# Load gates that register no readers, scratch stores on GpSimd's queue, transposes on SP's queue alone, and scale rows spread from columns

## The reference

```python
h = rmsnorm(x, norm1_g)
z = h @ w_in                       # 1536 columns: a (pool) | u | v
a = z[:, :512]; u = gelu(z[:, 512:1024]); v = gelu(z[:, 1024:])
pool = einsum((trailing_mean(a, windows 2/4/8/16) - a), pool_w) * pool_scale
gate = u * (masked(gmlp_ws) @ v + gmlp_b)      # chunks of 128 positions
x = x + concat(pool, gate) @ w_out
f = rmsnorm(x, norm2_g) @ w_up                 # 4096 columns
x = x + square(relu(f)) @ w_down
y = rmsnorm(x, normf_g)
```

## Time and profile before

| | us |
|---|---|
| median of 3 runs | 1406.8 (1393.67 to 1419.03) |
| the profiled execution | 1400.45 |
| span of its slowest core (core 2) | 1398.9 |
| spans of the 8 cores | 1372.8 to 1398.9 |
| PE busy | 1245.1 (89% of the span) |
| DVE, ACT, POOL busy | 556.3, 377.9, 47.0 |

### The profile page before, as it was taken

One profiled execution on the slowest core, in us unless ns is written; L12 is line 12 of the kernel. 1 busy time (PEld: TensorE's weight loads), 2 busy tenths in 40 slices (PEclk: granted clock), 3 DMA queues, 4 the chain that ended last, 5 costly groups with the idle time before them and its releaser, 6 DMA issues.

```text
span 1398.9 us, 18963 instructions; the slowest of 8 cores (1372.8 to 1398.9 us)
## 1 busy us (share of the span) xinstructions
PE 1245.1 (89%) x6628; PEld 648.8 (46%) x6628; DVE 556.3 (40%) x1165; ACT 377.9 (27%) x735; POOL 47.0 (3%) x91
## 2 busy tenths in 40 slices
PE   1688850499999999999999999999999999999996
PEld 0343420245545545545545545544554554554552
DVE  1764410234445336435435434442542443362312
ACT  0233200112224224223323323322431431421311
POOL 1010000000000000000000000000000000000000
PEclk6698975699999999999999999999999999999998
DMA  7996899847458349469448449549538637747751
GB/s 159 196 244 167 67 116 26 138 113 167 133 153 303 154 139 255 151 190 277 151 145 279 163 145 262 181 144 239 204 143 228 217 137 221 195 152 207 251 211 46
DMA packets 104605, 247.16 MB, mean 177 GB/s; under 512 B 70592, under 2 KB 70784, under 8 KB 81728
## 3 DMA queue, kind: packets, MB, share of 16 engines
q1 hardware_dynamic: 82224, 191.12, 44.4%
q0 software_dynamic: 12784, 52.47, 16.5%
q10 hardware_dynamic: 9504, 2.36, 5.8%
HBM read 218.07 MB, written 34.43 MB: 181 GB/s over the span
## 4 chain that ended last, share of the span: by engine, by line
PE 82%; another core or an unknown queue 4%; DVE 4%; DMA 3%; ACTq 3%; issue 2%; ACT 1%; SPq 1%; DVEq 0%; POOL 0%; POOLq 0%
PE ps L756 26%; PE ps L738 25%; PE ps L447 8%; PE ps L621 7%; PE ps L700 6%; PE ps L720 5%; PE ps L481 4%; ACTq L341 3%; DMA WAU<-w_au 1%; DMA H2T<-HB 1%; DMA RING<-xt 1%; ACT JUNK L306 1%; PE ps L576 1%; DVE X L779 0%
## 5 line engine op out<-in xcount | busy, mean ns | idle before, releaser
L738 PE MATMUL ps<-H2T,RING 128*128 128x384 bf16 x2304 | 387.6, 326 | 1.2 <-ACT ST L742 0.7
L756 PE MATMUL ps<-RING,ST 128*128 128x512 bf16 x1728 | 374.9, 379 | 0.0
L738 PEld LDWEIGHTS ps<-H2T,RING 128*128 128x128 bf16 x2304 | 224.1, 98 | 149.6 <-issue 2.0
L756 PEld LDWEIGHTS ps<-RING,ST 128*128 128x128 bf16 x1728 | 169.0, 98 | 202.5
L306 ACT ACTIVATE JUNK<-X 128x1024 bf16<-128x1024 f32 x93 | 98.3, 1057 | 468.7 <-DVE SS L303 225.1
L447 PE MATMUL ps<-HT,WAU 128*128 128x384 bf16 (+1 forms) x640 | 111.7, 337 | 90.7 <-DMA HT<-HB 61.0
L742 ACT ACTIVATE ST<-ps 128x384 bf16<-128x384 f32 x288 | 136.1, 491 | 188.4 <-PE ps L738 186.1
L744 DVE TENSOR_TENSOR ST<-ST 128x384 bf16<-128x384 bf16 x288 | 95.2, 355 | 168.3 <-ACT ST L742 167.9
L447 PEld LDWEIGHTS ps<-HT,WAU 128*128 128x128 bf16 x640 | 64.2, 101 | 136.9 <-issue 98.0
L621 PE MATMUL ps<-WOUT,MIXT 128*128 128x512 bf16 x480 | 108.1, 386 | 3.0 <-DVE MIXT L595 1.6
L761 DVE TENSOR_TENSOR X<-ps,X 128x512 f32<-128x512 f32 x54 | 37.1, 691 | 183.4 <-PE ps L756 183.4
(11 more groups left out here) (111 smaller groups left out, 660.8 us busy)
## 6 DMA issues: line engine op xcount, KB each, us to landing
RING<-scr SPq DMA_DIRECT2D x144, 1024.0 KB, 5.3
RING<-w_mlp POOLq DMA_DIRECT2D x16, 1024.0 KB, 14.5
scr<-RING SPq DMA_DIRECT2D x16, 1024.0 KB, 10.2
yall<-X POOLq DMA_DIRECT2D x30, 512.0 KB, 7.7
X<-xall POOLq DMA_DIRECT2D x27, 512.0 KB, 7.0
X<-xall SPq DMA_DIRECT2D x6, 512.0 KB, 23.5
WAU<-w_au POOLq DMA_DIRECT2D x4, 512.0 KB, 11.9
WOUT<-w_out POOLq DMA_DIRECT2D x2, 1024.0 KB, 34.6
```

The source lines that it names most:

```text
L738: i_ = e.matmul(bank(ub)[:, 0:TOK], lhsT=RING[s][:, k, (m % 4) * 128:(m % 4 + 1) * 128], rhs=H2T[:, k, :], start=(k == 0), stop=(k == 7))
L756: i_ = e.matmul(bank(n)[:, :], lhsT=ST[:, kg * 8 + kk, n * 128:(n + 1) * 128], rhs=RING[s][:, kk, :], start=(kg == 0 and kk == 0), stop=(k ...
```

## The change

- Prog.add gets `after`: the instruction waits for the last writer of these keys, but is not put down as a reader of them. All load gates use it, and the loads of XT1 now stand behind those of WAU in program order, so that they wait for the first piece of WAU.
- flush_stores issues the stores to the scratch on GpSimd's queue instead of SP's.
- All transposes are issued by SP.
- The sums of squares are made as columns (narrow matmuls against one column of ones, ONE1) for both blocks; norm_rs works on the columns, with a second call for the 16 halo tokens of block 0; a matmul of each column, broadcast along 128, with an identity (IDF, a new input of 64 KB) spreads it to a row, and ScalarE copies the row from PSUM to RSB.
- The order of the first WI_au groups, sums and evacuations is written anew, with 30 warming matmuls instead of 18.

```diff
-    def add(self, eng, fn, reads=(), writes=(), dma=None):
-        waits = []
+    def add(self, eng, fn, reads=(), writes=(), dma=None, after=()):
+        waits = [self.lastw[k] for k in after]
...
+        add("sp", lambda e: e.dma_start(out=IDF[:], in_=ident[:, :]), writes=["IDF"], dma="su0")
...
         for m in range(0, 8, 2):
             add("pool", lambda e, m=m: e.dma_start(out=WAU[:, m:m + 2], in_=w_au[:, m:m + 2]),
-                reads=[("XT0", 1)], writes=[("WAU", m), ("WAU", m + 1)], dma=f"wau{m}")
+                after=[("XT0", 1)], writes=[("WAU", m), ("WAU", m + 1)], dma=f"wau{m}")
+        for j in range(4):
+            add("sp", lambda e, j=j: e.dma_start(out=XT[1][:, 2 * j:2 * j + 2, :], in_=xt1[:, 2 * j:2 * j + 2, :]),
+                after=[("WAU", 0)], writes=[("XT1", j)], dma=f"xt1_{j}")
...
         def gen_first_sum(s):
...
+            fc = next_front()
+            kd = "1" if s == 0 else "2"
+
+            def col(e):
+                for n in range(NT):
+                    i_ = e.matmul(bank(fc)[:, n:n + 1], lhsT=SQ[:, 0, 16 * h + n * 128:16 * h + (n + 1) * 128], rhs=ONE1[:],
+                                  start=True, stop=True)
+                if h:
+                    i_ = e.matmul(bank(fc)[0:16, NT:NT + 1], lhsT=SQ[:, 0, 0:16], rhs=ONE1[:], start=True, stop=True)
+                return i_
+            add("pe", col, reads=["ONE1", key], writes=[("BANK", fc)])
+            norm_rs(kd, 0, NT, src=fc)
+            if h:
+                norm_rs(kd, NT, NT + 1, 16, src=fc)
+            return lambda: gen_first_row(s, kd)
+
+        def gen_first_row(s, kd):
...
+            def row(e):
+                if h:
+                    e.matmul(bank(fr)[:, 0:16], lhsT=RS[kd][0:16, NT:NT + 1].to_broadcast([16, 128]), rhs=IDF[0:16, 0:16],
+                             start=True, stop=True)
+                for n in range(NT):
+                    i_ = e.matmul(bank(fr)[:, 16 * h + n * 128:16 * h + (n + 1) * 128],
+                                  lhsT=RS[kd][:, n:n + 1].to_broadcast([128, 128]), rhs=IDF[:], start=True, stop=True)
+                return i_
+            add("pe", row, reads=["IDF"] + [("RS", kd, n) for n in range(NT + h)], writes=[("BANK", fr)])
+            add("act", lambda e: e.activation(out=R, in_=bank(fr)[:, 0:16 * h + TOK], func=AF.Copy), writes=[("BANK", fr), rk])
...
         def gen_N2_T(i, n0=0, n1=NT):
-            q = "act" if i < 2 else "sp"
+            q = "sp"
...
         def flush_stores():
             while pending_stores:
                 s_, q_ = pending_stores.pop(0)
-                add("sp", lambda e, s_=s_, q_=q_: e.dma_start(out=scr[q_], in_=RING[s_]),
+                add("pool", lambda e, s_=s_, q_=q_: e.dma_start(out=scr[q_], in_=RING[s_]),
...
-        gen_warm(18)
+        gen_warm(30)
         gen_first_x(0)
         gen_WI_au(0, 0, 1)
-        gen_first_sum(0)
+        row = gen_first_sum(0)
+        gen_WI_au(0, 1, 2)
+        row()
         late.pop(0)()
-        gen_WI_au(0, 1, 2)
         gen_first_x(1)
-        gen_first_sum(1)
-        gen_WI_au(0, 2, 8)
+        late.pop(0)()
+        gen_WI_au(0, 2, 3)
+        row = gen_first_sum(1)
+        gen_WI_au(0, 3, 4)
+        row()
+        for m in range(4, 8):
+            gen_WI_au(0, m, m + 1)
+            late.pop(0)()
...
-                gen_N1_T(2, "act")
+                gen_N1_T(2)
```

More of the change, by code:

```diff
@@ L142, in build_nc @@
     gf = din("normf_g", [D])
+    ident = din("ident", [128, 128])
     invc = din("invc", [128, 64])
@@ L183, in build_nc @@
         JUNK = sb("JUNK", [128, D], BF16)
-        ONES = sb("ONES", [128, 128], F32)
+        ONE1 = sb("ONE1", [128, 1], F32)
+        IDF = sb("IDF", [128, 128], F32)
         G1T = sb("G1T", [128, 8], F32)
@@ L242, in build_nc @@
         add("dve", lambda e: e.memset(WSMTS[:], 0.0), writes=["WSMTS"])
-        add("dve", lambda e: e.memset(ONES[:], 1.0), writes=["ONES"])
+        add("dve", lambda e: e.memset(ONE1[:], 1.0), writes=["ONE1"])
         add("dve", lambda e: e.memset(WSMT[64:128, :, 0:64], 0.0), writes=["WSMTz"])
@@ L249, in build_nc @@
                 writes=[("XT0", j)], dma=f"xt0_{j}")
+        add("sp", lambda e: e.dma_start(out=IDF[:], in_=ident[:, :]), writes=["IDF"], dma="su0")
         add("sp", lambda e: e.dma_start(out=INVC[:], in_=invc[:, :]), writes=["INVC"], dma="su6")
         add("sp", lambda e: e.dma_start(out=PSC[:], in_=pool_scale[:, :]), writes=["PSC"], dma="su5")
-        for j in range(4):
-            add("sp", lambda e, j=j: e.dma_start(out=XT[1][:, 2 * j:2 * j + 2, :], in_=xt1[:, 2 * j:2 * j + 2, :]),
-                reads=[("WAU", 0)], writes=[("XT1", j)], dma=f"xt1_{j}")
         def load_x(b, gate):
@@ L259, in load_x @@
                 add("sp", lambda e, n=n, t=t: e.dma_start(out=X[b][:, n, :], in_=xall[t * 128:(t + 1) * 128, :]),
-                    reads=[gate], writes=[("X", b, n)], dma=f"xld{b}sp_{n}")
+                    after=[gate], writes=[("X", b, n)], dma=f"xld{b}sp_{n}")
         def gen_L(i):
@@ L284, in build_nc @@
                                         in_=gmlp_b.rearrange("g c -> (g c)").partition_broadcast(128)),
-            reads=[("WV", 0)], writes=["BB"], dma="sb0")
+            after=[("WV", 0)], writes=["BB"], dma="sb0")
         load_x(0, ("WV", 0))
         load_x(1, ("WOUT", 0))
-        add("sp", lambda e: e.dma_start(out=G2B[:], in_=g2.partition_broadcast(128)), reads=[("WOUT", 0)], writes=["G2B"], dma="su3")
-        add("sp", lambda e: e.dma_start(out=G1B[:], in_=g1.partition_broadcast(128)), reads=[("WOUT", 1)], writes=["G1B"], dma="su1")
+        add("sp", lambda e: e.dma_start(out=G2B[:], in_=g2.partition_broadcast(128)), after=[("WOUT", 0)], writes=["G2B"], dma="su3")
+        add("sp", lambda e: e.dma_start(out=G1B[:], in_=g1.partition_broadcast(128)), after=[("WOUT", 1)], writes=["G1B"], dma="su1")
         def gen_setup_late():
@@ L354, in build_nc @@
         RSB = [X[2][:, 0, 0:W0], X[2][:, 2, 0:TOK]]
-        VRB = [X[2][:, 0, 512:512 + W0], X[2][:, 2, 512:512 + TOK]]
-        NWB = [X[2][:, 1, 0:W0], X[2][:, 1, 512:512 + TOK]]
         RSk = [("X", 2, 0), ("X", 2, 2)]
@@ L393, in gen_first_sum @@
             SQ = XT[0] if s == 0 else SQ1
-            W = W0 if s == 0 else TOK
+            h = 1 if s == 0 else 0
             key = ("XT0", 0) if s == 0 else ("ST", 8)
[L396 to L418, removed]
@@ L419, in gen_first_sum @@
-            if s == 0:
-                norm_rs("1", 0, NT, src=fc)
-            else:
+            fc = next_front()
[7 more added lines that the diff above has]
+                return i_
@@ new lines, in gen_first_sum @@
+            add("pe", col, reads=["ONE1", key], writes=[("BANK", fc)])
[4 more added lines that the diff above has]
+        def gen_first_row(s, kd):
+            h = 1 if s == 0 else 0
+            R, rk = RSB[s], RSk[s]
+            fr = next_front()
+            def row(e):
[8 more added lines that the diff above has]
+            add("act", lambda e: e.activation(out=R, in_=bank(fr)[:, 0:16 * h + TOK], func=AF.Copy), writes=[("BANK", fr), rk])
+            if s == 1:
@@ L967 @@
         "norm2_g": np.ascontiguousarray(np.asarray(norm2_g, f32)[0]),
+        "ident": np.eye(128, dtype=f32),
         "normf_g": np.ascontiguousarray(np.asarray(normf_g, f32)),
```

## The result

The changed kernel takes 1358.17 us (median of 4 runs, 1356.46 to 1364.38) against 1408.92 for the kernel before on the same chip: a ratio of 0.9683, 95% interval 0.9596 to 0.9769. The forecast was 1360, in a range of 1308 to 1422. The profiled execution took 1356.46, with a span of 1354.9 on core 0, so 44 us less than the 1400.45 against which the sum was made.

What follows compares the result with a forecast made beforehand. PE was taken as busy from 265 us on, so only waits before that counted: late start loads and transposes slowed beside GpSimd's converting loads. 1400 - 5 (start) - 35 (stall) = 1360 us, range 1308 to 1422.

Steps and rivals of the forecast that it cites:

- The start: New load gates and scale rows: WI_au(1), block 1's first multiplication, at 46 to 47 instead of 67.19, 20 us sooner.
- Given back: First N2 transposes (H2T), issued near 100 us, meet full DMA queues: of the 20 us won earlier, 5 are kept.
- Transposes on SP: Block 2's transposes issued from 156.5 instead of 161.54, first 1056 packets ahead of ring load 5: 24 us sooner.
- Stores on GpSimd: Sixteen scratch stores: issue costs nothing; GpSimd's waits leave fewer loads beside the transposes, 11 us, against more MB on q0.
- the two-load limit: GpSimd waits for load k, stores it, then issues load k+2: two loads in flight instead of four, 11 us.
- the stall: PE's 59.09 us wait for block 2's transposes until 264.74, before WI_au(2): to shrink by 35 us, between 0 and 74.
- The ring supply: Ring loads during the stores' waits: five slots cover the delay, costing nothing, or up to 10 us without that cover.
- The sum: Whole kernel: 1400 less 5 for the start and 35 for the stall makes 1360 us.
- B: Rival: which queue issues makes no difference and the stall stays; 1385 to 1400 us, chance 0.24.
- C: Rival: block 2's transposes on SP land in about 10 us; 1303 to 1330 us, chance 0.20.
- D: Rival: GpSimd's waits become the bound, deciding from about 30 us a load; 1420 to 1440 us, chance 0.16.
- The sentence on being wrong at the root: The prediction called itself wrong at the root if the collapse beside the transposes needs SP's stores as a third queue.

Runs made afterwards that it cites:

- x2: The changed kernel with stores back on SP and transposes of blocks 0 to 2 back on ACT, so load gates and scale rows alone: ratio 0.9943.
- x5: x4 with, in addition, ring load 3 held until H2T's transposes have landed, and load 4 and the late setup until block 2's have: 1305.1 us, ratio 0.9322.
- x7: The changed kernel with only the scratch stores back on SP, transposes staying on SP: 1366.83 us, ratio 0.9741.
- x1: The changed kernel with the transposes of blocks 0 to 2 back on ACT, stores staying on GpSimd: 1342 us, ratio 0.9544.
- x9: The kernel before, with each ring load issued only when the load two before it has landed: 1375.43 and 1394.74 us, ratio 0.9903.
- x10: The changed kernel with each scratch store issued one load later, so up to three ring loads are in flight: 1351.2 us, ratio 0.9658.
- x4: The changed kernel with ring load 5 held until block 2's transposes have landed, these placed ahead of block 1's UP groups: 1323.84 us, ratio 0.9422.
- x6: The kernel before with w_mlp handed in as bf16, so ring loads need no conversion and read half the bytes: 1349.21 us, ratio 0.9636.
- x11: x5 with the scratch stores back on SP: 1304.81 and 1305.37 us, ratio 0.9355.
- x12: The kernel before with the edits of x5 (both holds, block 2's transposes earlier) and nothing of the change: 1328.09 and 1333.24 us, no ratio.
- x8: The changed kernel with each ring load and scratch store cut into four transfers, packets 2 KB instead of 8 KB: 1344.74 us, ratio 0.9598.

## Why the prediction came out right, point by point

**The start** was right in its steps and near in its numbers. WI_au(1) was put at 46 to 47 and started at 49.28; XT1 went out at 16.06, where 14.5 was taken, and its last piece was squared from 36.06, where 33 was taken. The new norm, put at near 6 us, took 5.5, from the column matmuls at 38.84 to the scaling at 44.33.

**Given back**: right. H2T's transposes were put at 100 and are issued at 99.12; UP was put at 128 if nothing is kept and starts at 127.39. Of the 20 us, 1.2 are kept where 5 were taken. x2 prices the start at 0.6%, and x5 shows what it needs to be kept: H2T's transposes free of ring loads, 6.3 us from issue to UP instead of 28.3.

**Transposes on SP**: this step failed. The argument was that an issue at 156.5 puts the first 1056 packets ahead of load 5, against 645 by 170 us in the trace. They were issued at 155.51, and only 371 packets had passed by 160; from there on they took turns with q0. What the move is worth depends on where the stores are, which the prediction did not ask. With the stores on SP it gives 2.0%, some 28 us (x7 against x2), near the 24 that were summed, but not by the earlier issue: x7's transposes go out at 161.35, 1.4 us ahead of x2's, and behind a store on the same queue. With the stores on GpSimd it gives nothing: with the transposes left on ACT (x1) the kernel is not slower but, if anything, 1.4% faster. In the change as it is, then, the 24 us were not the gain of this step.

**Stores on GpSimd**: the right part was credited for the wrong reason. The sum took the two-load limit as the gain (11 us) and the stores' own MB on q0 as a load against it. Limit alone: 0.9903, the stall stays (x9). Limit relaxed: 0.9658, the gain stays (x10). What pays is where the stores go: moving them alone, with the transposes on ACT, takes 0.9943 to 0.9544 (x2 and x1), some 56 us, where 11 were summed. With the transposes already on SP it adds nothing that shows (0.9741 in x7, 0.9683 with it; the intervals overlap). The ring supply, costed at nothing, was nothing: PE does not wait for RING.

**The sum** was 35 for the stall; it measured 53.3 at WI_au(2), of which 9.3 were given back later. The 53.3 hold the 1.2 that the start kept, where 5 were summed beside the 35; so 44 came out where 40 were forecast: two misses of opposite sign, and two terms added that do not add. That the total came so near is luck. The end of the stall was put at 230 and came at 211.45, by a mechanism half right: the collapse does depend on what runs beside the transposes, but not on the time of issue (in x1 they are issued at 160.51, and WI_au(2) does not wait for HT), and not in the main on the number of loads in flight (x9).

**The rivals.** B, that the queue makes no difference, is refuted by x1 against x2, and again by x7 against x2. The rule of the Trainium skill named there ("DMA: Bandwidth & Descriptors", "Issuing engines are not separate DMA queues") does not hold for this stage: moving the stores between issuers, with nothing else changed, is worth some 56 us (x1 against x2), and little of that is issue time, since sixteen issues of 0.54 us on GpSimd make 9. The measurement decides. C, transposes on SP in 10 us, needed them alone: x4 has it, in 3.93 us of issue. D, GpSimd's waits as the bound, did not come: loads 7 and 8 landed in 19.3 and 19.0 us, not 65.4, under the 30 from which it was to decide. The sentence on being wrong at the root is half true: the stall to 256 us and more was seen only with SP's stores as a third queue beside converting loads, as the prediction feared, but x7 has a collapse of the rate, to 67 GB/s, between two queues.

**What stays open** is why converting loads without stores among them run so slowly beside transposes. x6 says that conversion or the bytes it reads take part, x11 and x12 that loads and stores without transposes do not have it. No run here tells whether it is the order of the packets or the place where they go, nor why single packets then keep their engine so long. Nor is it shown why one move makes the other worth nothing.

## What to carry to other kernels

In these runs transposes in packets of 256 B that took turns with packets of 8 KB got through when the other queue ran dry, whoever issued them: so look at what else is queued at the moment, and either hold those transfers for the few microseconds (x4, x5: 6.8% against 3.2% for the move of the queues) or cut them into smaller packets (x8). A start that comes 18 us sooner into full DMA queues kept 1 us; free the queues first. A forecast may land on the number with the wrong cause: only the kernels that do one half each (x1, x2, x7, x9, x10) told what paid. And two halves of a change can each give nearly the whole gain, so that removing one at a time makes either look worthless: run all four.

## What the runs showed of the hardware

- Three transposes of 128 x 1024 take 3.9 us to issue with nothing beside them (x4) and 51.8 beside a full q0, at 28 to 30 packets a microsecond of 8 KB packets, or 84 of 2 KB packets (x8).
- All queues together beside transposes, from 182 to 200 us: 220 GB/s with loads and stores in one queue, 164 with the stores on SP (before, which fell to 24 from 210 to 230), 67 with no store on the move (x7). Loads and stores on two queues without transposes: 195 from 170 to 180 us (x12).
- In the crawl the packets last longer, by share and count: a transpose packet 0.7 us from 210 to 230 us of before, against 0.04 in the changed kernel and 0.02 alone.
- An engine blocked in a DMA issue can act as a brake: in x1 ACT's 38 us kept a load back for 18 us, and WI_au(2) started 6.6 us sooner than in the changed kernel. That the one made the other is read from the timeline, not tested by itself.
